# Hyena stage of a hybrid encoder layer: the signal spectra use two pairs of PSUM banks in turn, and all other units rotate over four banks

## The reference, cut to what matters

```python
def _long_conv(z, h_fwd, h_bwd, skip):
    length = z.shape[1]
    kcirc = jnp.concatenate([h_fwd, jnp.zeros((1, c), jnp.float32), h_bwd[:0:-1]], axis=0)
    zf = z.astype(jnp.float32)
    spec = jnp.fft.rfft(zf, n=2 * length, axis=1) * jnp.fft.rfft(kcirc, axis=0)[None]
    y = jnp.fft.irfft(spec, n=2 * length, axis=1)[:, :length]
    return y + zf * skip.astype(jnp.float32)
...
    zz = hx1.astype(f32) * _long_conv(hv, filt[:, 0, 0], filt[:, 0, 1], skip[0])
    zz = hx2.astype(f32) * _long_conv(zz, filt[:, 1, 0], filt[:, 1, 1], skip[1])
```

## Time and profile before

| what | value |
|---|---|
| median of 3 runs | 2813.46 us (2810.33 to 2817.49) |
| profiled execution | 2810.5 us |
| its span | 2808.7 us, mean granted TensorE clock 0.970 |
| PE busy | 2598.6 us (93%) |
| DVE, ACT, POOL busy | 1645.1 us, 950.2 us, 579.4 us |
| hyena stage, long item 2 | 51.21 us from its first K matmul to that of the next item |
| hyena stage, wide items 9 and 10 | 40.95 us each |

### The profile page before, as it was taken

The page is one execution under the profiler, slowest core; times in us unless marked ns, Lnnn a source line. Parts: engine busy times, 40 slices in busy tenths (PEclk is TensorE's granted clock), DMA queues, the critical chain, the costliest instruction groups (busy, mean ns, idle before and its releaser), DMA issues.

```text
span 2808.7 us, 35773 instructions
## 1 busy us (share of the span) xinstructions
PE 2598.6 (93%) x14020; PEld 1503.3 (54%) x14020; DVE 1645.1 (59%) x2273; ACT 950.2 (34%) x1803; POOL 579.4 (21%) x526
## 2 busy tenths in 40 slices
PE   6989797989999989999789999999988999999997
PEld 3434332346676757666665565556533444444486
DVE  5746455646666757554558878856785243633453
ACT  5322122224545545454533333333342122311232
POOL 0103233421121222122233534513210000000000
PEclk9999898999999999999989999999999999999999
DMA  5724564343343434242542332343632030100032
GB/s 208 258 71 184 198 241 153 131 150 123 122 158 132 159 123 151 106 149 102 201 162 105 135 135 94 132 146 139 203 122 96 30 105 1 61 30 31 31 101 88
DMA packets 153311, 355.73 MB, mean 127 GB/s; under 512 B 8121, under 2 KB 110757, under 8 KB 146488
## 3 DMA queue, kind: packets, MB, share of 16 engines
q1 hardware_dynamic: 134360, 245.03, 25.5%
q0 software_dynamic: 18640, 102.11, 9.4%
q10 hardware_dynamic: 144, 6.29, 0.7%
HBM read 221.19 MB, written 138.51 MB: 128 GB/s over the span
## 4 chain that ended last, share of the span: by engine, by line
PE 38%; DVE 10%; issue 3%; DMA 2%; ACT 1%; POOL 0%; DVEq 0%; ACTq 0%; POOLq 0%
PE ps L1292 26%; PE ps L1535 5%; PE ps L1480 3%; DVE mem L2257 3%; PE ps L1473 2%; PE ps L1553 1%; DVE mem L2448 1%; DMA s_og<-mem 1%; DMA s_ks<-mem 0%; DVE mem L2350 0%; DVE mem L2331 0%; DVE mem L2335 0%; DVE mem L2334 0%; DVE mem L820 0%; DMA s_hy<-mem 0%
## 5 line engine op out<-in xcount | busy, mean ns | idle before, releaser
L1292 PE MATMUL ps<-mem 128*128 128x512 f16 (+1 forms) x9312 | 1760.0, 349 | 27.6 <-ACT mem L1746 11.5
L1292 PEld LDWEIGHTS ps<-mem 128*128 128x128 f16 x9312 | 931.4, 103 | 829.0 <-issue 98.4
L839 ACT ACTIVATE mem<-mem 128x2048 f16<-128x2048 f32 (+1 forms) x56 | 108.7, 1940 | 405.7 <-DVE mem L857 405.5
L2157 DVE TENSOR_TENSOR mem<-ps,mem 128x512 f32<-128x512 f32 (+2 forms) x144 | 79.6, 553 | 206.2 <-PE ps L1421 187.9
L1473 PE MATMUL ps<-mem 128*128 128x512 f32 x384 | 176.0, 599 | 26.2 <-DVE mem L2257 22.6
L1480 PE MATMUL ps<-mem 128*128 128x512 f16 (+1 forms) x1080 | 193.2, 337 | 0.0
L827 POOL PARTITION_ALL_REDUCE mem<-mem x56 | 38.1, 682 | 721.2 <-DVE mem L820 675.5
L864 DVE SCALAR_TENSOR_TENSOR mem<-mem 128x2048 f16<-128x2048 f32 (+1 forms) x56 | 129.7, 2317 | 78.6 <-ACT mem L839 78.6
L1535 PE MATMUL ps<-mem 128*128 128x256 f32 x768 | 169.5, 380 | 0.0
L1765 ACT ACTIVATE mem<-ps 128x512 f32<-128x512 f32 (+1 forms) x144 | 71.9, 500 | 282.9 <-PE ps L1434 282.4
L2205 DVE TENSOR_TENSOR mem<-mem 128x1024 f16<-128x1024 f32 x96 | 144.6, 1506 | 32.4 <-ACT mem L1784 32.1
(11 more groups left out here) (195 smaller groups left out, 2629.6 us busy)
## 6 DMA issues: line engine op xcount, KB each, us to landing
s_ks<-mem SPq DMA_DIRECT2D x96, 512.0 KB, 2.6
mem<-s_ks SPq DMA_DIRECT2D x24, 2048.0 KB, 8.7
mem<-in_w_in SPq DMA_DIRECT2D x44, 1024.0 KB, 5.4
s_uc<-mem POOLq DMA_DIRECT2D x24, 768.5 KB, 6.7
mem<-s_uc SPq DMA_DIRECT2D x18, 1024.0 KB, 6.1
s_sums<-mem POOLq DMA_DIRECT2D x16, 1024.0 KB, 4.4
s_taps<-mem POOLq DMA_DIRECT2D x8, 2048.0 KB, 9.3
mem<-s_sums SPq DMA_DIRECT2D x32, 512.0 KB, 3.9
```

Of the source, the lines that this page charges most:

```text
L839: act.activation(w_place(b)[:, 0, 0:chunks(b)], raw_of(b), ACT.Copy, scale=wscale[b % 3]).then_inc(S["w_hi"], 1)
L1292: mm = pe.matmul(out, lhs(a, k), rhs(b, k), start=(k == 0 and x == 0), stop=(k == kc - 1 and x == 2))
```

## The change

Z units now use banks 4 and 5 for planes 0 and 2 and banks 6 and 7 for planes 1 and 3, in long and in wide items. All other units rotate over banks 0 to 3.

```diff
         def take(n):
-            return [place(next(turns) % 6) for _ in range(n)]
+            return [place(next(turns) % 4) for _ in range(n)]
...
                 if what == "K":
                     uk[i].update({n: take(1)[0] for n in kernel_units(p)})
-                elif wide(i) and p % 2:
-                    uz[i][2 * p:2 * p + 2] = take(2)
                 else:
-                    uz[i][2 * p:2 * p + 2] = [place(6), place(7)]
+                    uz[i][2 * p:2 * p + 2] = [place(4 + 2 * (p % 2)), place(5 + 2 * (p % 2))]
```

## The result

| | before | changed | predicted |
|---|---|---|---|
| median | 2815.02 us (4 runs) | 2788.38 us (4 runs, 2782.70 to 2792.03) | 2783.9 (2777 to 2798) |
| ratio of the runs | 1 | 0.9906, 95% interval 0.9883 to 0.9928 | 0.9895 |
| span of the profiled execution | 2808.7 us | 2780.9 us | 2779.1 |
| hyena stage, first T matmul to first L1292 (L1290) | 1418.63 to 2003.02, 584.39 us | 1423.71 to 1976.58, 552.87 us | 29.6 less |

The kernel became 0.9% faster, which is more than the 0.3% that a measurement of this kernel can tell from no change. In the stage itself 31.5 us are gone; the span shows 27.8 of them, since in this execution the stage also began 5.1 us later and the rest after it took 1.4 us less. The changed file is two lines shorter, so every line behind the edit has a number lower by two: L1473 is L1471 here, L1480 is L1478, L1553 is L1551, L2257 is L2255, L2330 is L2328.

A forecast was written before the change was run, and what follows sets the result against it. PE was taken as the kernel's bound, in a loop with DVE in long items. A gain of 32.6 us less 3.0 for load waits left 29.6: span 2779.1, median 2783.9 us, range 2777 to 2798.

The forecast's parts named there:

- What bounds the stage: Long items: PE loops with DVE through inverse, recombination, products and Z3 around one bank pair; Z waits total 25.0 us.
- Rival C: Long items: DVE needs its 8.13 us of idle time, the period stays 51.21, no gain, 2813.5 us; chance 0.07.
- The size per item: Long items: without Z waits T starts 25.39 us after the item's start, 4.36 us sooner; 32.6 us over all.
- The margin: Long items: the DVE loop would take 45.16 us, 1.7 us below PE's own 46.85, so PE is the limit.
- The ring of four: Banks 0 to 3: each unit needs the copy of the unit four back, formerly six; costed at nothing.
- Rival D: Ring: PE waits until a whole round of four is copied, 1.0 us each, 73 us lost, 2857 us; chance 0.05.
- the thin place from T to I: Ring's tightest place: the first I unit needs the first T unit's copy, with 0.45 us to spare.
- The loads: T in items 3 and 7 would wait 0.3 and 2.2 us for signal loads; 3.0 us subtracted from the gain.

The follow-up runs named there:

- experiment 1: Changed kernel with long items back on one Z bank pair, ring of four kept; ratio to before 1.0002, stage 584.49 us against 584.39.
- experiment 2: Kernel before with one repeated DVE subtraction in each recombination of a long item; median 2829.52 us against 2817.23, ratio 1.0045.
- two doses: Changed kernel with T behind the inverse's first half, plus two added subtractions per long-item recombination (2.90 us per item); long items 48.06 us against 46.85.
- experiment 5: Kernel before with the T units moved behind the first half of the inverse; median 2804.24 us against 2811.76, ratio 0.9968.
- experiment 3: Changed kernel with one repeated DVE subtraction in each recombination of a long item; median 2790.99 us, ratio to before 0.9905, stage 6.4 us longer.
- experiment 6: Changed kernel with T behind the inverse's first half, plus one added subtraction per long-item recombination; stage 547.04 us, 3.8 longer than without the subtraction.

## Why the prediction was right

**What bounds the stage.** PE and DVE in a loop around one bank pair: shown from three sides. A second pair removes all 30 waits, the ring alone removes none (experiment 1), and extra DVE work costs its full length in the kernel before although DVE idles there (experiment 2). Rival C, that DVE needed its idle time, falls with the row of 3.74 us.

**The size per item.** Predicted 25.39 us to T, a period of 46.85 and idle time of 3.8 on DVE; measured 25.39, 46.85 and 3.74. The estimate from the wide item's waitless run, not from the idle times in brackets, is what made it exact: brackets alone gave 3.35 instead of 4.36.

**The margin.** The loop's limit was put at 1.7 us below PE's; two doses found 1.69 free.

**The ring of four.** Costed at nothing; measured 0.1 us of stage. Rival D, rounds of the ring at 1.0 us each, is refuted down to a ring of two, which lost 17.6 us where D had 73 for a ring of four. At three banks a long item begins to pay, 0.19 us, so the thin place from T to I is real but covered by the fourth bank. The Trainium skill (Perfetto Trace Analysis, Matmul Optimizations) asks for all eight banks to be used. The runs agree only in part: banks 4 and 5 gave nothing as part of the ring and everything as a second pair for Z.

**The loads, the one term that was mis-sized.** I subtracted 3.0 us, 0.55 of it for item 3 and 2.46 for item 7. T waited 0.29 in item 3 as forecast, and 0.28 in item 7. There the load was issued 8.86 us after product 0 began, not 10.47 as in the trace of before, because the store ahead of it landed in 8.5 us and not in 10.1. The row of before was no accident of one execution: the two other kernels whose long items take 51.2 us (experiments 1 and 5) show 10.0 and 9.9 us at this place, and the nine profiles with another period 8.4 to 8.7. So the step that was off is that a landing time was carried over to a kernel in which everything around that store starts at other moments. Why the time differs was not tested. Load waits took 1.1 us instead of 3.0, and that is why the stage gained 31.5 and not 29.6.

**From the stage to the median.** The gain is 31.5 us in the stage, 27.8 in the span and 26.6 in the medians, so the median came out 4.5 us above the forecast although the stage gained more than forecast. The time that is missing was not given back behind the stage: in the twelve profiles of this study the part behind it took between 804.1 and 806.1 us. It is the part ahead that moves: the first T matmul stood between 1415.27 and 1431.88 us, though none of the kernels changes anything there. The two profiles in which it stood latest (1428.47 and 1431.88) also have the lowest mean granted clock, 0.966 and 0.964 against 0.969 to 0.971 in the other ten; that the two go together is all that is shown. So medians of a few runs differ by some us for reasons outside the stage, and stage times from the trace are the better measure of an edit.

**What stays open.** Why the part ahead of the stage varies was not tried, and neither was why the store in item 7 lands sooner in the changed kernel. Nor was it tried whether Z2's wait of 1.1 us in item 8 can be moved; it is the last wait of a Z matmul.

## What to carry to other kernels

When an engine waits for the release of a buffer, count for every class of buffers how long one is in use, from the first matmul until it is read, against how long it takes to fill. The pair of a wide item was in use for 5.14 us and filled in 3.44. An I bank was in use for 2.6 us and filled in 1.7 (from the row of I at 1554.15 to the end of ACT's copy at 1556.74). Both classes need two by this count; the ring's third and fourth bank cover T, whose units are shorter than their copies, and two of its six banks were idle capacity. Price the gain from a stretch in which the same instructions run without waits, and look at once for what is late next: the loads had nothing to spare where the products had 1.8 us, and moving their reader by one block took another 9.7 us from the stage. Idle time of an engine in a loop is not slack; a dose of extra work tells the two apart.

## What was not expected of the hardware

Matmuls behind a wait sometimes ran slowly, and the length of the wait alone does not say when. After a wait of 5.21 us T took 3.68 us and not 1.91, as in the trace of before, with a granted clock of 0.50, which is the lower of TensorE's two levels, 1.2 GHz. After a wait of 1.95 us it took 3.50 with a clock of 0.53 (experiment 3). After a wait of 2.58 us on a Z matmul of item 8 the 16 matmuls took 8.80 us in experiments 2 and 6, and 7.11 us in experiment 3. After 2.5 us at Z1 they ran slowly in three of seven long items of experiment 2 and at full clock in the other four. So a wait can cost 1.8 times its length in one place (1.95 + 1.59 us) and its own length in the next. Behind the waits of 0.99 to 1.74 us inside the stage no group was slow in any of these runs.

The store of 1 MB to HBM landed in 8.2 to 10.0 us in the changed kernel with the same instruction each time. That spread is larger than the margins that a load behind it has here.
